# Decoder step with a mixture of experts: the way from routing to the first expert reordered, the overflow branch moved behind the last expert

## The chip, the cores and the metric

One Trainium2 chip, one of its cores. The metric is device time in microseconds (us) of one execution; lower is better. Engines: TensorE (PE; PEld is its weight load), VectorE (DVE), ScalarE (ACT), GpSimd (POOL), SyncE (SP, which only issues DMAs).

## The reference, cut to what matters

544 tokens (512 of a prompt, 32 of a sample group), width 1024, all fp32. After attention, convolution and memory attention each token has a row h; hn is h normalised. A router picks 4 of 32 experts per token, and each expert is a clamped SwiGLU:

```python
logits = (x @ w_router) + b_router                 # x = rmsnorm(h), 544 rows
top_v, top_e = lax.top_k(logits, 4)
gates = softmax(top_v)
h_ = xb @ w_gate_up[e] + b_gate_up[e]              # per expert, on its own tokens
gate = minimum(h_[:, 0::2], 7); up = clip(h_[:, 1::2], -7, 7)
y_e = ((up + 1) * gate * sigmoid(1.702 * gate)) @ w_down[e] + b_down[e]
y = rmsnorm(h + sum over the 4 experts of gates * y_e) * g_final
```

## The kernel before, in words

The kernel has two stages. The first, up to about 235 us, computes h and hn, row tile by row tile (4 tiles of 128 tokens, one of 32), and writes them to two tables in DRAM, y_tbl and hn_tbl (SP, lines 517 and 519). The second goes through the 32 experts, each as one block of at most CAP = 104 tokens. If an expert has more tokens, 20 more blocks are computed at the end; the 0/1 value flag_i says whether any has. With the inputs timed here it is 0.

Between the stages stands the routing. For expert 0, VectorE writes the one-hot matrix hot (which token sits in which slot, line 1526). TensorE multiplies it by the token numbers (line 2441). VectorE turns the result into row numbers idx_i (line 1641). GpSimd gathers these rows of hn_tbl with an indirect DMA (gather, line 737). TensorE transposes the gathered rows (x_rows, line 2355), ScalarE rounds them to the high part (x_high, line 1127), and VectorE computes the low part (x_low, line 1754). Then TensorE begins the products of expert 0. The weight of each token in its sum, its gate, is computed on VectorE by gates (lines 1510 to 1513, 1500, 1501), brought into slot order by a second product with hot (info, line 2342; for expert 0 line 2447) and reduced by slot_info (line 1658) to the column gcol. For later experts slot_info also writes the row numbers (line 1657).

An expert's weights are 12 halves of 128x2048 fp32. A 2 MB chunk (two halves) comes by one SP DMA (line 444) into one of 6 buffers. For each half ScalarE makes the high part (high_part, line 1098, one of 4 buffers), VectorE the low part (low_part, line 1690: raw minus high), and TensorE does three products for each piece (lines 2371 to 2373: high times high, high times low, low times high), 12 products for a half of gate_up. The code numbers the halves 0 to 11 within a period; the periods before the first, with n = -1, hold halves 10 to 13, which are the first four halves of expert 0. So gate_up(-1, 10) is the first product of the second stage, and low_part(-1, 10) the low part that it needs.

The order on every engine is written out by hand: head(0), then period(n) for each expert, with semaphores between engines. head(0) on VectorE is slot_info(0, 0), low_part 10, hot_slots(1, 1) (line 1648), x_low(0), low_parts 11, 12 and 13, and slot_info(1, 1), which gives the row numbers of expert 1. x_rows(1) comes on TensorE after the sixth half of period 0.

Before head(0) every engine reads flag_i into a register (value_load), behind the semaphore route_ready. VectorE branches on it: the overflow code (some 200 instructions) or one memset (line 1745). Then it sets route_ready (line 1748). "spare" (line 1910) is a product of the identity with itself that nobody reads; one shows as two instructions.

Of the kernel before, what the change touches and what calls it, by code (L numbers as in the profile page):

```python
# [112 lines left out]
def build(nc, x_prompt, x_sample, mem_prompt, cache_win_k, cache_win_v, win_kT, mem_kT, cache_mem_v,  # L113
# [4 lines left out]
    with ctx:  # L118
# [174 lines left out]
        ssl, rsl = small[:, 190:192], small[:, 192:194]  # L293
        sink8 = small[:, 172:182]
# [128 lines left out]
        def _(sp):  # L423
# [106 lines left out]
            sp.wait_ge(sem("route_ready"), 1)  # L530
            flag = sp.value_load(flag_i[0:1, 0:1], min_val=0, max_val=1)
# [31 lines left out]
            with sp.Fori(2, NE // UB - 1) as it:  # L563
                for u in range(UB):
                    refills(it * UB + u)
            for n in range(NE - UB, NE - 2):
                refills(n)
# [25 lines left out]
            with sp.If(flag > 0):  # L593
                sp.wait_ge(sem("st_y"), 16 * NTT)
                sp.wait_ge(sem("ld_yl"), 16)
                e = sp.value_load(eid_i[0:1, 0:1], min_val=0, max_val=NE - 1)
# [32 lines left out]
        def _(pool):  # L629
# [63 lines left out]

            pool.wait_ge(sem("group_pe"), 2)
# [14 lines left out]

            bound = pool.alloc_register("bound")  # L710
            pool.wait_ge(sem("eid_zero"), 1)
            none = pool.value_load(eid_i[0:1, EXTRA:EXTRA + 1], min_val=0, max_val=0)
# [74 lines left out]
            pool.wait_ge(sem("gates_ready"), 3)  # L787
            head(0)
            pool.wait_ge(sem("route_ready"), 1)
            flag = pool.value_load(flag_i[0:1, 0:1], min_val=0, max_val=1)  # L790
# [31 lines left out]

            for u in range(UB):
                period(NE - UB + u, u, u == UB - 1, u < 2, u == 2)
# [3 lines left out]
            with pool.Else():  # L828
                head(NE)
# [8 lines left out]
        def _(ac):  # L838
# [299 lines left out]
            def head(m):  # L1138
                if m:
                    for i in (10, 11, 12):  # L1140
                        high_part(m - 1, i, True)
                else:
                    ac.wait_ge(sem("pos_pe"), NTT + 2)
                bias_seed(m, 0)
                x_high(m)
                high_part(m - 1, 13, True)
                bias_seed(m, 1)
                high_part(m - 1, 14, True)
                bias_seed(m, 2)
                bias_seed(m, 3)  # L1150
# [60 lines left out]
            for par, n in ((0, 3), (1, 2)):  # L1211
                ac.wait_ge(sem(f"st_h{par}"), 16 * n)
                ac.wait_ge(sem(f"st_hn{par}"), 16 * n)
            for i in (10, 11, 12):
                high_part(-1, i, True)
            ac.wait_ge(sem("route_ready"), 1)
            flag = ac.value_load(flag_i[0:1, 0:1], min_val=0, max_val=1)
# [3 lines left out]
            with ac.Fori(2, NE // UB - 1) as it:  # L1221
                for u in range(UB):
                    period(it * UB + u, u)
            for u in range(UB):
                period(NE - UB + u, u, u == UB - 1)
# [5 lines left out]
            with ac.Else():  # L1231
                ac.wait_ge(sem("w_used"), NE * HALVES)
                head(NE)
# [14 lines left out]
        def _(dv):  # L1248
# [390 lines left out]
            gates(NTT - 2, NTT - 1, P, 2)  # L1639
            dv.wait_ge(sem("pos_pe"), NTT + 1)  # L1640
            v.tensor_scalar(idx_i[0:CAP, 0:1], banks[6][0:CAP, 416:417], float(NT), None, ALU.add).then_inc(sem("idx_ready"), 1)
            gates(NTT - 1, NTT, NSM, 3)
# [49 lines left out]
            link(v.tensor_copy(cnt, banks[0][:, 160:192]))  # L1692
            link(v.tensor_reduce(wk[:, 9, 0:1], cnt, AX.X, ALU.max))
            link(v.tensor_scalar(wk[:, 9, 1:2], wk[:, 9, 0:1], CAP + 0.5, None, ALU.is_gt))
            link(v.tensor_copy(flag_i[:, :], wk[:, 9, 1:2]))
            flag = dv.value_load(flag_i[0:1, 0:1], min_val=0, max_val=1)

            with dv.If(flag > 0):

                for par, n in ((0, 3), (1, 2)):  # L1700
                    dv.wait_ge(sem(f"st_hn{par}"), 16 * n)
                c0 = chain[0]
# [39 lines left out]

                skipped = chain[0] - c0
            with dv.Else():
                v.memset(eid_i[:, 0:EXTRA], 0).then_inc(sem("dve_chain"), skipped)
            dv.wait_ge(sem("dve_chain"), chain[0])

            v.memset(mx, 0.0).then_inc(sem("route_ready"), 1)
# [27 lines left out]

            def head(m):
                if m:
                    for i in (10, 11):
                        low_part(m - 1, i, True)  # L1780
                if not m:
                    slot_info(0, 0, again=False)
                    low_part(m - 1, 10, True)
                else:
                    hot_slots(m, 0)
                    slot_info(m, 0)
                hot_slots(m + 1, 1)
                x_low(m)
                if not m:
                    low_part(m - 1, 11, True)  # L1790
# [48 lines left out]
            def period(n, k, last=False, table=False, bare=False):  # L1839
                old = not (last or table or bare)  # L1840
                for i in range(10 if last else HALVES):
# [13 lines left out]
                    if not last or i + 2 < 10:  # L1855
                        low_part(n, i + 2, last)
                    if i == 0 and old:
# [18 lines left out]
            head(0)  # L1876
            for u in range(2 * UB):
                period(u, u)
            with dv.Fori(2, NE // UB - 1) as it:
                for u in range(UB):  # L1880
                    period(it * UB + u, u, table=True)
            for u in range(UB):
# [4 lines left out]
            with dv.Else():  # L1887
                dv.wait_ge(sem("w_used"), NE * HALVES)
                head(NE)
# [14 lines left out]
        def _(pe):  # L1904
# [440 lines left out]
            def x_rows(n, k):  # L2345

                pe.wait_ge(sem("gathered"), n * 16 + 16)
                if isinstance(n, int) and n in (0, NE):
# [57 lines left out]
            def head(m):  # L2406
                if m:
                    info(m, 0)
                x_rows(m, 0)
                pe.wait_ge(sem("x_low"), m * 2 + 2)  # L2410
                gate_up(m - 1, 10, True, 0)
                gate_up(m - 1, 11, True, 0)
# [48 lines left out]
            for u in range(UB):  # L2461
                period(NE - UB + u, u, u == UB - 1, u < 2, u == 2)
            with pe.If(flag > 0):
                head(NE)
# [56 lines left out]
```

## Time and profile before

| what | value |
|---|---|
| median of 3 runs | 1386.02 us (1385.52 to 1387.04) |
| the profiled execution | 1385.96 us |
| its span in the trace | 1384.1 us |
| mean granted TensorE clock | 0.995 |
| TensorE busy | 1352.9 us (98% of the span) |
| VectorE, ScalarE, GpSimd busy | 1209.8, 1091.7, 1010.1 us |
| DMA, mean | 332 GB/s |

The profiled execution took 1.9 us more than its span; that part lies outside the first and last instruction. Positions in the trace are given as microseconds from the start of the span. A busy time is the union of the engine's instructions. In the chain, each piece is what released the next.

### The profile page before, as it was taken

Reading aid. Unit: us, or ns where it says so; the run is one execution under the profiler, and the core shown is the slowest. Engines: PE = TensorE matmul, PEld = TensorE weight load, DVE = VectorE, ACT = ScalarE, POOL = GpSimd, SP = SyncE. Lnnn points to the kernel's source line nnn. Section 1 sums busy time; section 2 is a strip of 40 time slices with the busy share of each in tenths; the row PEclk is TensorE's granted clock in tenths of the full one; section 3 lists DMA queues with packets and bytes.
Section 4 is the critical chain, followed back from the end, with each engine's and each line's share of the span. In section 5 each row is a group of like instructions: output and inputs, shape, how many; then the busy total and the mean of one; then the engine's idle time right before and its main releaser. Section 6 shows DMA issues by size and latency. Waiting matters only on the chain.

```text
span 1384.1 us, 19701 instructions
## 1 busy us (share of the span) xinstructions
PE 1352.9 (98%) x6762; PEld 994.0 (72%) x6762; DVE 1209.8 (87%) x1092; ACT 1091.7 (79%) x1149; POOL 1010.1 (73%) x431
## 2 busy tenths in 40 slices
PE   8999999999999999999999999999999999999995
PEld 5988655667777777777777777777777777777773
DVE  5466556899999999999999999999999999999996
ACT  5354423778888888888888888888888888888885
POOL 2122211266699999899999998999999989999943
PEclk9999999999999999999999999999999999999998
DMA  9522272999999999999999999999999999999984
GB/s 354 189 66 72 88 276 70 367 394 356 372 351 377 378 369 382 372 392 379 377 393 373 378 382 375 379 384 365 389 380 365 381 390 374 382 371 386 375 313 150
DMA packets 51803, 458.99 MB, mean 332 GB/s; under 512 B 11450, under 2 KB 15516, under 8 KB 26122
## 3 DMA queue, kind: packets, MB, share of 16 engines
q1 hardware_dynamic: 40089, 438.33, 80.9%
q0 software_dynamic: 10000, 18.19, 6.0%
q10 hardware_dynamic: 1648, 1.65, 0.4%
q8 instruction: 36, 0.59, 0.2%
q14 instruction: 30, 0.24, 0.0%
HBM read 446.62 MB, written 22.08 MB: 339 GB/s over the span
## 4 chain that ended last, share of the span: by engine, by line
PE 77%; DMA 3%; DVE 1%; issue 1%; POOL 1%; ACT 0%; POOLq 0%; ACTq 0%; DVEq 0%
PE psum L2371 24%; PE psum L2373 24%; PE psum L2372 24%; DMA area<-hn_tbl,idx_i 3%; PE psum L2355 2%; PE psum L2366 2%; POOL small L810 0%; DVE low L1690 0%; PE psum L2342 0%; DVE area L1812 0%; POOL area L695 0%; DVE area L1772 0%; DVE ring L1836 0%; DVE area L1765 0%; POOL out L820 0%
## 5 line engine op out<-in xcount | busy, mean ns | idle before, releaser
L1690 DVE TENSOR_TENSOR low<-raw,high 128x2048 fp32r<-128x2048 f32 x384 | 875.1, 2310 | 35.9 <-ACT high L1098 35.8
L1098 ACT CAST high<-raw 128x2048 fp32r<-128x2048 f32 x384 | 727.8, 1913 | 23.7 <-PE psum L2373 19.2
L2371 PE MATMUL psum<-high,area_r 128*104 128x512 f32 x1536 | 610.4, 397 | 2.5 <-DVE area_r L1754 1.4
L2373 PE MATMUL psum<-low,area_r 128*104 128x512 f32 x1536 | 604.3, 393 | 0.0
L2372 PE MATMUL psum<-high,area_r 128*104 128x512 f32 x1536 | 603.9, 393 | 0.0
L668 POOL PARTITION_BROADCAST brow<-brow x192 | 382.8, 2074 | 41.1 <-DMA brow<-in_biases 40.6
L2373 PEld LDWEIGHTS psum<-low,area_r 128*104 128x104 f32 x1536 | 258.0, 168 | 96.5
L2371 PEld LDWEIGHTS psum<-high,area_r 128*104 128x104 f32 x1536 | 258.0, 168 | 95.0 <-DVE area_r L1754 1.6
L2372 PEld LDWEIGHTS psum<-high,area_r 128*104 128x104 f32 x1536 | 258.3, 168 | 90.7
L737 POOL DMA_INDIRECT area<-hn_tbl,idx_i x32 | 162.9, 5089 | 79.5 <-DVE idx_i L1657 40.8
L665 POOL COPY arrived<-cst 1x1 f32 x60 | 199.5, 3325 | 0.3
L747 POOL DMA_INDIRECT y_tbl<-area,idx_i x31 | 160.1, 5164 | 12.7 <-issue 6.4
L1136 ACT COPY psum<-brow 104x512 f32<-104x512 f32 x192 | 110.9, 589 | 4.9 <-POOL brow L668 4.1
L645 POOL TENSOR_TENSOR ring<-ring,small 128x512 f32<-128x512 f32 (+2 forms) x18 | 24.2, 1358 | 80.4 <-DVE small L1364 80.4
L1122 ACT CAST area_r<-psum 128x416 fp32r<-128x416 f32 x64 | 32.4, 505 | 58.4 <-PE psum L2366 58.4
L1112 ACT ACTIVATE area<-psum,cst 104x512 f32<-104x512 f32 x64 | 44.1, 688 | 31.8 <-PE psum L2373 31.8
L721 POOL DMA_INDIRECT slot_tbl<-wr,us x20 | 58.0, 2899 | 5.4 <-issue 5.4
L2129 PE MATMUL psum<-ring,area 128*128 128x512 f32 x112 | 52.4, 601 | 0.0
L728 POOL CAST idx_i<-us 104x1 int32 (+1 forms) x22 | 19.3, 876 | 43.0 <-PE psum L2373 43.0
L1118 ACT ACTIVATE area<-area,cst 104x512 f32<-104x512 f32 x64 | 47.0, 735 | 2.7
L1106 ACT ACTIVATE area<-psum,area 104x512 f32<-104x512 f32 x62 | 39.3, 685 | 12.5 <-PE psum L2373 12.5
L1759 DVE TENSOR_TENSOR area_r<-psum,area_r 128x416 fp32r<-128x416 f32 x64 | 37.6, 588 | 11.7 <-ACT area_r L1122 11.6
(269 smaller groups left out, 1175.5 us busy)
## 6 DMA issues: line engine op xcount, KB each, us to landing
raw<-in_w_gate_up SPq DMA_DIRECT2D x128, 2048.0 KB, 11.1
raw<-in_w_down SPq DMA_DIRECT2D x64, 2048.0 KB, 11.7
ring<-in_w_in SPq DMA_DIRECT2D x7, 1024.0 KB, 15.3
ring<-in_x_prompt SPq DMA_DIRECT2D x8, 512.0 KB, 9.7
ring<-in_w_out SPq DMA_DIRECT2D x7, 512.0 KB, 4.6
ring<-in_w_mem_kv SPq DMA_DIRECT2D x2, 1024.0 KB, 9.3
ring<-in_mem_kT SPq DMA_DIRECT2D x1, 2048.0 KB, 8.5
ring<-in_cache_mem_v SPq DMA_DIRECT2D x1, 2048.0 KB, 8.2
```

Of the source, the lines that this page charges most:

```text
L665: nc.gpsimd.tensor_copy(arrived[0:1, part:part + 1], seen[:, bass.ds(n, 1), 0])
L668: nc.gpsimd.partition_broadcast(brow[:, cols], brow[0:1, cols], channels=P).then_inc(sem("bias_cast"), 1)
L721: nc.gpsimd.indirect_dma_start(slot_tbl[:, :], bass.IndirectOffsetOnAxis(ap=slot_i[0:n, i:i + 1].bitcast(U32), axis=0), slot_row[0:n, i, : ...
L737: nc.gpsimd.indirect_dma_start(xg[0:CAP, k % 2, :], None, hn_tbl[:, :], bass.IndirectOffsetOnAxis(ap=idx_i[0:CAP, k % UB:k % UB + 1].bitca ...
L747: nc.gpsimd.indirect_dma_start(y_tbl[:, :], bass.IndirectOffsetOnAxis(ap=idx_i[0:CAP, (k - 1) % UB:(k - 1) % UB + 1].bitcast(U32), axis=0) ...
L1098: nc.scalar.copy(high_w(i), raw_w(t)).then_inc(sem("w_high"), 1)
L1136: nc.scalar.copy(banks[q][0:CAP, :], brow[0:CAP, q * 512:(q + 1) * 512]).then_inc(sem("spare_bias_in"), 1)
L1690: v.tensor_tensor(low_w(t), raw_w(t), high_w(i), ALU.subtract).then_inc(sem("w_low"), 1)
L2129: last = mm(bank[0:n, :], zT[:, t, j * P:j * P + n], wo[t][:, half * 512:(half + 1) * 512], start=(t == tiles[0]), stop=(t == tiles[-1]))
L2371: mm(bank, high, wh, start=False, stop=False, skip_group_check=True)
L2372: mm(bank, low, wh, start=False, stop=False, skip_group_check=True)
L2373: return mm(bank, high, wl, start=False, stop=stop, skip_group_check=True)
```

## The change

It has six parts. One thing serves them all: `counted`, a semaphore set by the copy of the counts.

1. The flag is read late. On ScalarE, VectorE, GpSimd and SP the read stands before the last four experts, on TensorE after the last. VectorE computes it there (overflow_flag). The overflow code moves into the branch at the end.
2. GpSimd reads the constant `none` before it clears xg, not between the arrival of hn_tbl and the gather. It no longer waits for gates_ready.
3. ScalarE starts the high parts when VectorE has written hn (hn_ready), not when the stores of h and hn have landed. It waits for gates_ready before high part 13.
4. VectorE copies the counts out of PSUM, writes the row numbers of expert 0, and then goes: low_part 10, low_part 11, gates of the last two row tiles, x_low(0), hot_slots(1, 1), low_part 12, slot_info(0, 0), low_part 13; slot_info(1, 1) follows the first low part of period 0.
5. TensorE does the six wide products that stood behind route_ready behind `counted`, and the product of the gates (info(0, 0)) between the first and the second half of expert 0.
6. 12 spare products stand before the transposes of expert 0 (where 8 stood, and 5 stay ahead), and 6 between them and the first half.

```diff
 # sp
-            sp.wait_ge(sem("route_ready"), 1)
-            flag = sp.value_load(flag_i[0:1, 0:1], min_val=0, max_val=1)
...
+            sp.wait_ge(sem("flag_ready"), 1)
+            flag = sp.value_load(flag_i[0:1, 0:1], min_val=0, max_val=1)
 # gpsimd
+            bound = pool.alloc_register("bound")
+            pool.wait_ge(sem("eid_zero"), 1)
+            none = pool.value_load(eid_i[0:1, EXTRA:EXTRA + 1], min_val=0, max_val=0)
             pool.wait_ge(sem("group_pe"), 2)
             nc.gpsimd.memset(xg, 0.0).then_inc(sem("zeroed"), 1)
...
             for par, n in ((0, 3), (1, 2)):
                 pool.wait_ge(sem(f"st_hn{par}"), 16 * n)
-
-            bound = pool.alloc_register("bound")
-            pool.wait_ge(sem("eid_zero"), 1)
-            none = pool.value_load(eid_i[0:1, EXTRA:EXTRA + 1], min_val=0, max_val=0)
...
             gather(0, 0)
-            pool.wait_ge(sem("gates_ready"), 3)
             head(0)
-            pool.wait_ge(sem("route_ready"), 1)
-            flag = pool.value_load(flag_i[0:1, 0:1], min_val=0, max_val=1)
 # scalar
                 x_high(m)
+                if not m:
+                    ac.wait_ge(sem("gates_ready"), 3)
                 high_part(m - 1, 13, True)
...
-            for par, n in ((0, 3), (1, 2)):
-                ac.wait_ge(sem(f"st_h{par}"), 16 * n)
-                ac.wait_ge(sem(f"st_hn{par}"), 16 * n)
+            ac.wait_ge(sem("hn_ready"), NTT + 1)
             for i in (10, 11, 12):
                 high_part(-1, i, True)
-            ac.wait_ge(sem("route_ready"), 1)
-            flag = ac.value_load(flag_i[0:1, 0:1], min_val=0, max_val=1)
             head(0)
 # vector
             first_slots(NTT - 2, NTT).then_inc(sem("hot_ready"), 1)
-            gates(NTT - 2, NTT - 1, P, 2)
+            v.tensor_copy(cnt, banks[0][:, 160:192]).then_inc(sem("counted"), 1)
             dv.wait_ge(sem("pos_pe"), NTT + 1)
             v.tensor_scalar(idx_i[0:CAP, 0:1], banks[6][0:CAP, 416:417], float(NT), None, ALU.add).then_inc(sem("idx_ready"), 1)
-            gates(NTT - 1, NTT, NSM, 3)
...
+            def first_head():
+                low_part(-1, 10, True)
+                low_part(-1, 11, True)
+                gates(NTT - 2, NTT - 1, P, 2)
+                gates(NTT - 1, NTT, NSM, 3)
+                x_low(0)
+                hot_slots(1, 1)
+                low_part(-1, 12, True)
+                slot_info(0, 0, again=False)
+                low_part(-1, 13, True)
...
+                    if isinstance(n, int) and n == 0 and i == 0:
+                        slot_info(1, 1)
...
-            head(0)
+            first_head()
...
+            overflow_flag()
+            dv.wait_ge(sem("flag_ready"), 1)
+            flag = dv.value_load(flag_i[0:1, 0:1], min_val=0, max_val=1)
 # tensor, head(0)
                 x_rows(m, 0)
+                if not m:
+                    for _ in range(6):
+                        mm(banks[5][:, 0:P], ident, ident, start=False, stop=True, skip_group_check=True)
                 pe.wait_ge(sem("x_low"), m * 2 + 2)
                 gate_up(m - 1, 10, True, 0)
+                if not m:
+                    pe.wait_ge(sem("gates_ready"), 3)
+                    info(0, 0)
                 gate_up(m - 1, 11, True, 0)
 # tensor, before head(0)
             spare(5, banks[1], ident)
-            pe.wait_ge(sem("gates_ready"), 3)
+            pe.wait_ge(sem("counted"), 1)
+            for q in range(6):
+                last = mm(banks[q][0:CAP, :], hot[:, 0, 0, :], hot[:, 0].rearrange("p j s -> p (j s)")[:, 0:512], start=True, stop=True)
+            last.then_inc(sem("pos_pe"), 1)
             pe.wait_ge(sem("idx_ready"), 1)
-            for j in range(NTT):
-                last = mm(banks[6][0:CAP, 416:420], hot[:, 0, j, :], rv_all[:, 0, j, :], start=(j == 0), stop=(j == NTT - 1))
-            last.then_inc(sem("info_pe"), 1)
-            spare(8, banks[1], ident)
-            pe.wait_ge(sem("route_ready"), 1)
-            flag = pe.value_load(flag_i[0:1, 0:1], min_val=0, max_val=1)
-            for q in range(6):
-                last = mm(banks[q][0:CAP, :], hot[:, 0, 0, :], rv_all.rearrange("p n j c -> p (n j c)")[:, 0:512], start=True, stop=True)
-            last.then_inc(sem("pos_pe"), 1)
+            spare(12, banks[7], ident)
             head(0)
```

## Rows read from the trace of the kernel before

**Rows 1.** The page: span, and busy time of each engine.
```profile
span 1384.1 us, 19701 instructions
PE 1352.9 (98%) x6762; PEld 994.0 (72%) x6762; DVE 1209.8 (87%) x1092; ACT 1091.7 (79%) x1149; POOL 1010.1 (73%) x431
```

**Rows 2.** The waits of TensorE from 262 us on: total, times, longest.
```profile
PE psum L2355 <- DMA area<-hn_tbl,idx_i: 3.6, 2, 3.0
```

**Rows 3.** The chain of waits, 228 to 262 us: start, duration, what.
```profile
236.96 0.50 POOLq L712
...
238.21 0.96 issue
239.17 5.17 DMA area<-hn_tbl,idx_i
...
246.69 0.48 PE psum L2371
...
254.03 0.39 PE psum L2342 x5
...
255.52 16.51 DMA area<-hn_tbl,idx_i
```

**Rows 4.** The timeline of VectorE around the first expert: start, duration, instruction.
```profile
234.15 0.73 DVE L1477 SCALAR_TENSOR_TENSOR area<-ring,small 32x512 f32<-32x512 f32 x1
...
235.63 0.18 DVE L1510 TENSOR_TENSOR ring<-ring 128x32 f32<-128x32 f32 x1
...
236.86 0.15 DVE L1641 TENSOR_SCALAR idx_i<-psum 104x1 int32<-104x1 f32 x1
...
237.97 0.21 DVE L1501 TENSOR_TENSOR area_r<-area,area_r 32x32 fp32r<-32x32 f32 x1
...
240.47 0.07 DVE L1745 MEMSET eid_i<- 128x20 int32 x1 [1.59 <-issue]
...
257.38 2.28 DVE L1690 TENSOR_TENSOR low<-raw,high 128x2048 fp32r<-128x2048 f32 x1
```

**Rows 5.** The timeline of ScalarE, same stretch.
```profile
234.26 0.23 ACT L994 ACTIVATE ring<-ring 32x32 f32<-32x32 f32 x1 [1.87 <-DVE ring L1495]
237.02 5.51 ACT L1098 CAST high<-raw 128x2048 fp32r<-128x2048 f32 x3 [2.54 <-DMA hn_tbl<-area]
```

**Rows 6.** The timeline of GpSimd: the gathers of experts 0, 1 and 2.
```profile
239.17 1.39 POOL L737 DMA_INDIRECT area<-hn_tbl,idx_i  x1 [4.95 <-issue]
255.52 5.10 POOL L737 DMA_INDIRECT area<-hn_tbl,idx_i  x1 [14.96 <-DVE idx_i L1657]
...
287.88 9.94 POOL L737 DMA_INDIRECT area<-hn_tbl,idx_i  x1 [12.79 <-PE psum L2373]
```

**Rows 7.** A later gather on GpSimd and VectorE beside it, in one timeline.
```profile
1222.27 5.68 POOL L737 DMA_INDIRECT area<-hn_tbl,idx_i  x1 [0.88 <-DMA brow<-in_biases]
...
1222.47 4.49 DVE L1690 TENSOR_TENSOR low<-raw,high 128x2048 fp32r<-128x2048 f32 x2
```

**Rows 8.** Stretches: length, busy time of PE, PEld, DVE, ACT, POOL; clock; DMA.
```profile
241.00:244.00 3.00, 1.63 (x6) 0.93 (x6) 2.55 (x2) 2.12 (x2) 0.00 (x0) 1.00 0.40 105
244.00:247.50 3.50, 1.74 (x12) 1.36 (x13) 1.96 (x3) 2.49 (x3) 0.00 (x0) 1.00 0.59 154
247.50:251.00 3.50, 3.50 (x10) 2.40 (x9) 3.50 (x3) 0.71 (x2) 0.00 (x0) 0.51 1.01 431
```

**Rows 9.** The timeline of TensorE: spare products, wide products, transposes.
```profile
238.72 2.03 PE L1910 MATMUL psum<-cst 128*128 128x128 f32 x16
241.59 1.63 PE L2453 MATMUL psum<-area_r 128*104 128x512 f32 x6 [0.85 <-DVE small L1748]
```

**Rows 10.** The timeline of VectorE at the change from expert 27 to 28.
```profile
1227.37 8.89 DVE L1690 TENSOR_TENSOR low<-raw,high 128x2048 fp32r<-128x2048 f32 x4
1237.59 2.29 DVE L1690 TENSOR_TENSOR low<-raw,high 128x2048 fp32r<-128x2048 f32 x1 [1.32 <-ACT high L1098]
```

**Rows 11.** The timeline of ScalarE, same stretch.
```profile
1240.03 0.69 ACT L1112 ACTIVATE area<-psum,cst 104x512 f32<-104x512 f32 x1 [0.67 <-PE psum L2373]
```

More of the change, by code:

```diff
@@ L293, in build @@
         ssl, rsl = small[:, 190:192], small[:, 192:194]
+        most = small[:, 194:196]
         sink8 = small[:, 172:182]
@@ L595, in _ @@
                 sp.wait_ge(sem("ld_yl"), 16)
+                sp.wait_ge(sem("route_ready"), 1)
                 e = sp.value_load(eid_i[0:1, 0:1], min_val=0, max_val=NE - 1)
@@ L821, in last_store @@
                                              bounds_check=bound, oob_is_err=False).then_inc(sem("st_last"), 16)
+            pool.wait_ge(sem("flag_ready"), 1)
+            flag = pool.value_load(flag_i[0:1, 0:1], min_val=0, max_val=1)
             for u in range(UB):
@@ L828, in _ @@
             with pool.Else():
+                pool.wait_ge(sem("route_ready"), 1)
                 head(NE)
@@ L1223, in _ @@
                     period(it * UB + u, u)
+            ac.wait_ge(sem("flag_ready"), 1)
+            flag = ac.value_load(flag_i[0:1, 0:1], min_val=0, max_val=1)
             for u in range(UB):
@@ L1232, in _ @@
                 ac.wait_ge(sem("w_used"), NE * HALVES)
+                ac.wait_ge(sem("route_ready"), 1)
                 head(NE)
@@ L1690, in low_part, with overflow_flag, overflow_blocks @@
                 v.tensor_tensor(low_w(t), raw_w(t), high_w(i), ALU.subtract).then_inc(sem("w_low"), 1)
[L1692 to L1702, printed above, removed]
+            def overflow_flag():
+                link(v.tensor_reduce(most[:, 0:1], cnt, AX.X, ALU.max))
+                link(v.tensor_scalar(most[:, 1:2], most[:, 0:1], CAP + 0.5, None, ALU.is_gt))
+                v.tensor_copy(flag_i[:, :], most[:, 1:2]).then_inc(sem("flag_ready"), 1)
+            def overflow_blocks():
                 nb, ci, cx, t0 = (wk[:, r, 0:NE] for r in (9, 10, 11, 6))
@@ L1741, in _ @@
                 link(gate_parts(P, 0, NTT, NE, NE + EXTRA))
[L1743 to L1748, printed above, removed]
+                v.memset(mx, 0.0).then_inc(sem("route_ready"), 1)
             def x_low(n):
@@ L1775, in swiglu @@
                 v.scalar_tensor_tensor(out=u, in0=u, scalar=1.0, in1=g, op0=ALU.add, op1=ALU.mult).then_inc(sem("glu_ready"), 1)
-            def head(m):
[L1778 to L1786, printed above, removed]
+            def first_head():
[8 more added lines that the diff above has]
+                low_part(-1, 13, True)
+            def head(m):
+                for i in (10, 11):
+                    low_part(m - 1, i, True)
+                hot_slots(m, 0)
+                slot_info(m, 0)
                 hot_slots(m + 1, 1)
                 x_low(m)
-                if not m:
-                    low_part(m - 1, 11, True)
                 low_part(m - 1, 12, True)
@@ L1888, in _ @@
                 dv.wait_ge(sem("w_used"), NE * HALVES)
+                overflow_blocks()
                 head(NE)
@@ L2347, in x_rows @@
                 pe.wait_ge(sem("gathered"), n * 16 + 16)
-                if isinstance(n, int) and n in (0, NE):
+                if isinstance(n, int) and n == NE:
                     pe.wait_ge(sem("gcol_ready"), counted(n) + 1)
@@ L2462, in _ @@
                 period(NE - UB + u, u, u == UB - 1, u < 2, u == 2)
+            pe.wait_ge(sem("flag_ready"), 1)
+            flag = pe.value_load(flag_i[0:1, 0:1], min_val=0, max_val=1)
             with pe.If(flag > 0):
+                pe.wait_ge(sem("route_ready"), 1)
                 head(NE)
```

## The prediction, made before the changed kernel ran

> **What bounds the kernel.** I read the page first. TensorE is busy for 1352.9 of 1384.1 us, 98%, and no other engine is above 87% [rows 1]. The reader is to see that a microsecond counts only if TensorE's stream of products starts earlier or waits less. Next I read TensorE's waits from 262 us on. Gathers end two of them, together 3.6 us, the longest 3.0 us [rows 2]. So the second stage is a nearly closed stream, and the change can gain or lose only at its start, in these waits, or by cutting a new hole.
>
> Then I read the chain around the start [rows 3]. The store of hn lands at 236.96, GpSimd reads its constant, the gather of expert 0 starts at 239.17 and lands 5.17 us later, at 244.34, and the first product starts at 246.69. From landing to first product are 2.35 us: transposes, high part, low part. The chain does not pass through the flag, the branch or the gates. The timelines show why: VectorE has its row numbers at 236.86 + 0.15 = 237.01 and is through the gates at 237.97 + 0.21 = 238.18 [rows 4], long before 244.34. The branch costs VectorE an idle 1.59 us [rows 4] and TensorE an idle 0.85 us before the wide products [rows 9], both under the gather's flight. Taking the flag away is by itself worth nothing on the chain.
>
> The windows add one thing. TensorE's clock was granted in full up to 247.5. From 247.5 to 251.0 it was at 0.51, the 1.2 GHz level, after the engine had been busy for 1.63 of 3.00 and 1.74 of 3.50 us [rows 8]. Half rate for 3.5 us costs about 1.7 us.
>
> **The parts, costed.**
>
> GpSimd's constant (part 2). Before, 2.21 us pass from 236.96 to the gather at 239.17, with the last 0.96 us "issue" [rows 3]. Without the load the issue stays: 237.92 and thus **-1.25 us** for the start. The row numbers don't hold it: with the gates moved behind them they come earlier than 237.01. The expert 1 gather shows the same distance: TensorE's product starts at 254.03 and takes 0.39 us, and 255.52 is 1.1 us after that [rows 3], with VectorE's 0.15 us instruction between.
>
> ScalarE and VectorE start sooner (parts 3 and 4). ScalarE's last small job ends at 234.49, and it then waits for the store until 237.02 [rows 5]. VectorE's last write of hn ends at 234.15 + 0.73 = 234.88 [rows 4]. So the high parts start near 234.9. Three take 5.51 us [rows 5], 1.84 each: done at 236.8, 238.6 and 240.4. VectorE then does low part 10 from 236.9 and low part 11 without a gap, to 241.4 (two in 4.49 us [rows 7]). In the first stage's end this looks free: VectorE was idle there.
>
> It is not free, because **the gather now starts inside these two low parts**. GpSimd's gather instruction takes 1.39 us for expert 0, when VectorE does nothing long, 5.10 us for expert 1 and 9.94 us for expert 2 [rows 6]. The reader should lay each beside VectorE's timeline. The gather of expert 1 starts at 255.52 and ends at 260.62; the low part that starts at 257.38 ends at 259.66 [rows 4], 0.96 us before. The gather at 1222.27 ends at 1227.95; the two low parts beside it end at 1226.96 [rows 7], 0.99 us before. Every gather I laid beside VectorE this way ends about 1.0 us after the first gap in a run of instructions that read two SBUF tiles. So the gather of expert 0 will start at 237.9, find its gap after low part 11 at about 241.5, and end at 242.5, where it ended at 240.56: **+1.95 us** (this holds the -1.25 us already). Its unknown is bounded by 1.39 us (not held, end at 239.3) and 9.94 us (end at 247.9). I take 4.6 us, because low part 11 is followed by the short instructions of the gates, which read one tile every second time.
>
> Here a page speaks. The Trainium skill, in "SBUF — State Buffer", section "Who interferes with whom", says that a tensor_tensor with two SBUF inputs contends with GpSimd's reads, and infers that writing the descriptors of a DMA is not touched by it. By its inference gathers would not be stretched by low parts, the landing would be near 243.1 and the kernel faster (second rival). The trace disagrees with the inference by 5.10 and 9.94 against 1.39 us [rows 6], and the measurement decides.
>
> From the end of the gather instruction to the landing were 244.34 - 240.56 = 3.8 us; the load is the same, so it lands at 246.3. With 2.35 us behind it the first product is at 248.6, **+1.95 us**. The gates take 237.97 + 0.21 - 235.63 = 2.55 us [rows 4], now from 241.4 to 244.0, before x_low needs VectorE at about 247.2: nothing. If the gather were quick they would end just before x_low: nothing to +0.3.
>
> Gates' product between the halves (part 5). Five short products took 0.39 us in the same place one half later [rows 3]: **+0.4 us** on TensorE. Below nothing is excluded, it is an addition; above, if gates or high part 13 were late, +1. High part 13 waits for x_high anyway.
>
> Spare products (part 6). Sixteen instructions took 2.03 us [rows 9], so a spare product is 0.25 us. The twelve, with five and the six wide products (1.63 us [rows 9]) before them, keep TensorE busy to about 242.3, and it then idles until 246.3: nothing on the chain. The six last 1.5 us inside the 1.4 us that TensorE waits for x_low: 0 to +0.1, up to +0.7 if the clock falls among them. The clock's part: before, 3.5 us at half rate all fell on products. Now TensorE idles for 4 us in one piece, so I expect the fall too, but the first 1.1 us of it on spare products: **-0.4 us**. The bounds are -1.7 (no fall) and +1.3 (a fall that starts with the products and lasts longer).
>
> slot_info(1, 1) behind a low part (part 4). It releases the gather of expert 1, 255.52 before. Counting on from a first product at 248.6: VectorE's low part 13 waits for slot_info(0, 0), so for TensorE, and the next low part ends near 257.3, the gather starts near 258.4. But now only one low part stands in its way, not one and a half, so its instruction ends at 261.4 against 260.62. TensorE reaches the transposes of expert 1 about 1.9 us later than before and had waited a little there. The gather lands 1 to 2 us later: they meet. I count **-0.1 us**. What is late next is the gather of expert 2, held 9.94 us [rows 6] and followed by the 3.0 us wait [rows 2]. It is started by VectorE's slot_info, which moves along with TensorE, so the wait stays: 0.
>
> The late flag (part 1). VectorE has four low parts from 1227.37 on without a gap; the third ends near 1234.0 and there the flag goes in: three short instructions, 0.6 us, and the load, 1.59 us [rows 4]. The fourth then ends at 1238.5, not 1236.26. After it VectorE idled 1.32 us [rows 10]. TensorE needs it when it has done the second half of expert 28, at 1240.03 [rows 11]. Cover 1.5 us: nothing; without the cover +0.7, on ScalarE's side too. SP and GpSimd have a half's time to spare. TensorE's load is behind its last product, and removing the branch on VectorE moves nothing as shown above.
>
> **The sum.** +1.95 + 0.4 - 0.4 - 0.1 = +1.85 us. Against the profiled execution, 1385.96 us, that is 1387.8. It stands 0.06 us from the median of 1386.02, so the forecast is 1387.8 for the median too. About 0.2%, or 2.8 us, is what a measurement of this kernel can tell from no change.
>
> **The rivals.**
>
> First, the forecast: the gather of expert 0 is held by the low parts. Chance 0.50.
>
> Second, it is not held (it gets in before VectorE, or a gap opens between the two low parts). Then -1.25 at the start, +0.4 for the gates' product, and no long idle, so the clock may stay full: up to -1.7. The sum is -2.5, of which the gather of expert 1 and the DMA traffic may take back one: 1383.5 to 1385, likeliest 1384. For it speaks that the forecast counts 1 us steps; against it all three gathers of rows 6. Chance 0.22.
>
> Third, it is held, but the shift opens a gap for the gather of expert 2. Its 9.94 us [rows 6] shrink and the 3.0 us wait [rows 2] goes: 1387.8 - 3.0 = 1384.8. Against it: VectorE, ScalarE and TensorE shift together. Chance 0.10.
>
> Fourth, the other side, slower beyond measurement: the clock. TensorE idles 4 us before the transposes. If the clock is at half from the transposes through the whole first half of weights, its 12 products take 5.1 us for 2.75, so 2.35 us are lost where 1.7 were, and the six spare products overrun by 0.7: +1.85 + 0.4 + 0.65 + 0.7 = +3.6, 1389.6. It decides from a fall before 246.5 on. Chance 0.12.
>
> Fifth, the late flag cuts a hole of 1 to 2 us: 1389. Chance 0.06.
>
> **How the numbers follow.** The likeliest case gives 1387.8. The range takes in the second and third rival and the fourth: 1383.2 to 1389.8. Faster by over 0.2% (below 1383.2) needs the second rival's best or two lucky ones: 0.14. Slower by over 0.2% (above 1388.8) is the fourth, part of the fifth and the worse bounds of the first: 0.19. The rest, 0.67, is within.
>
> **What would show it.** Right: the gather of expert 0 starts near 237.9 and its instruction lasts 4 to 5 us, ending 1 us after low part 11; the first product comes at 248 to 249; a clock stretch near 0.5 of 2 to 3.5 us; the 3.0 us wait is still there; no wait of TensorE near 1240. Wrong: a gather instruction of 1 to 2 us with landing at 243 (second rival), a gather of expert 2 much below 9.9 us (third), transposes of 0.2 us a piece (fourth).

## The result and the profile after

The changed kernel is slower: 1389.72 us median of 22 runs (1384.21 to 1391.95) against 1385.61 us (1383.92 to 1387.59, 22 runs) of the kernel before. The ratio is 1.0025, 95% interval 1.0017 to 1.0032, so +3.5 us; the two medians lie 4.1 us apart. The forecast was +1.85 us, 1387.8, in a range (1383.2 to 1389.8) that holds the median by 0.08 us; but I gave "within 0.2%" 0.67 and "slower" only 0.19, and slower it is.

The profiled execution took 1387.46 us, one of the quicker ones. The reader must know this before he compares the traces: it shows the start of the trouble and not its usual size. Among the 22 runs the mean granted clock goes with the time, but loosely: 1384.2 us at 0.996, 1387.1 to 1387.7 at 0.995, 1388.2 to 1390.8 at 0.992, 1390.1 to 1391.9 at 0.990; yet 1385.7 to 1389.6 at 0.994 and 1387.9 to 1392.0 at 0.991.

First the page of the changed kernel, then its chain around the first expert (start, duration, what).

```profile
span 1385.6 us, 19736 instructions
PE 1358.0 (98%) x6782; PEld 999.2 (72%) x6782; DVE 1209.6 (87%) x1090; ACT 1091.7 (79%) x1149; POOL 1000.5 (72%) x431
```

```profile
235.88 1.90 DMA hn_tbl<-area
...
238.37 0.96 issue
239.33 6.11 DMA area<-hn_tbl,idx_i
245.49 1.40 PE psum L2357 x8
246.89 2.53 PE psum L2414 x12
249.41 0.23 PE psum L2373
```

VectorE's timeline of the same execution:

```profile
235.12 0.73 DVE L1479 SCALAR_TENSOR_TENSOR area<-ring,small 32x512 f32<-32x512 f32 x1
...
237.94 4.49 DVE L1691 TENSOR_TENSOR low<-raw,high 128x2048 fp32r<-128x2048 f32 x2 [0.41 <-ACT high L1099]
...
246.77 1.28 DVE L1746 TENSOR_TENSOR area_r<-psum,area_r 128x416 fp32r<-128x416 f32 x2 [1.93 <-ACT area_r L1128]
```

TensorE's timeline:

```profile
245.49 1.40 PE L2357 MATMUL psum<-cst,area 104*128 104x104 f32 x8 [2.85 <-DMA area<-hn_tbl,idx_i]
...
249.14 0.51 PE L2373 MATMUL psum<-high,area_r 128*104 128x512 f32 x1
```

VectorE's last write of hn is at 235.12 where it was at 234.15 [rows 4]. This 0.97 us is there from about 20 us on, long before anything that the change touches, so I take it off ("stage 1 taken off" from here on). Then the gather starts at 238.4 instead of 239.17 [rows 3], lands at 244.5 instead of 244.34, and the first product is at 248.2 (249.14 in TensorE's timeline) instead of 246.69. From landing to first product were 2.35 us and are 3.7. The chain shows why: it now runs through the six spare products (L2414), which take 2.53 us. VectorE's x_low ends at 246.77 + 1.28 = 248.05, 1.1 us before the first product. The spares, meant for the wait for x_low, outlast it. The windows of the changed kernel (columns as in rows 8) show why:

```profile
244.00:247.50 3.50, 2.01 (x12) 2.02 (x13) 1.36 (x6) 1.08 (x3) 0.00 (x0) 0.76 0.44 87
247.50:251.00 3.50, 3.50 (x18) 3.05 (x17) 3.36 (x3) 2.22 (x2) 0.00 (x0) 0.76 0.90 365
```

The clock was at half from about 245.8 to 249.2, after TensorE had idled 2.85 us before the transposes. In the kernel before this stretch lay on products [rows 8]; here on transposes and spares. GpSimd's timeline, gathers of experts 0 to 2:

```profile
239.33 2.17 POOL L738 DMA_INDIRECT area<-hn_tbl,idx_i  x1 [3.82 <-issue]
258.10 2.96 POOL L738 DMA_INDIRECT area<-hn_tbl,idx_i  x1 [16.61 <-DVE idx_i L1658]
...
289.04 9.94 POOL L738 DMA_INDIRECT area<-hn_tbl,idx_i  x1 [12.80 <-PE psum L2375]
```

The gather of expert 0 took 2.17 us, more than 1.39 [rows 6] but far from 4.6. The question was whether this profile or my reckoning was the exception.

In the next section three executions in a slow state are left out everywhere: one of the changed kernel run again (2472.66 us) and two of the kernel without the six spares (2743.46 and 1500.97 us).

### The profile page after: what moved, and what is told of

The parts are those of the page before. It is cut to its first block, busy times and chain, and to the rows that moved or that the text cites. A ratio compares the mean times of both kernels' runs of the same rounds, so it can differ in the third digit from the quotient of the medians.

```text
span 1385.6 us, 19736 instructions
## 1 busy us (share of the span) xinstructions
PE 1358.0 (98%) x6782; PEld 999.2 (72%) x6782; DVE 1209.6 (87%) x1090; ACT 1091.7 (79%) x1149; POOL 1000.5 (72%) x431
## 4 chain that ended last, share of the span: by engine, by line
PE 88%; DVE 7%; issue 2%; DMA 1%; ACT 1%; POOL 1%; SPq 0%; POOLq 0%; DVEq 0%; ACTq 0%
PE psum L2373 23%; PE psum L2375 23%; PE psum L2374 23%; DVE low L1691 4%; PE psum L2131 4%; PE psum L1968 2%; PE psum L1970 2%; PE psum L1969 2%; PE psum L2357 2%; PE psum L2368 1%; PE psum L1933 1%; DMA ring<-in_w_mem_kv 1%; PE psum L1985 0%; PE psum L2065 0%; PE psum L2041 0%
## 5 line engine op out<-in xcount | busy, mean ns | idle before, releaser
L748 POOL DMA_INDIRECT y_tbl<-area,idx_i x31 | 157.3, 5075 | 12.1 <-issue 6.4
L1767 DVE SCALAR_TENSOR_TENSOR area<-area 104x512 f32<-104x512 f32 x64 | 45.9, 717 | 2.2
```

The source lines that it names most:

```text
L748: nc.gpsimd.indirect_dma_start(y_tbl[:, :], bass.IndirectOffsetOnAxis(ap=idx_i[0:CAP, (k - 1) % UB:(k - 1) % UB + 1].bitcast(U32), axis=0) ...
```

## The experiments

The expectations speak of two theories. Hold theory: GpSimd's gather instruction is kept waiting by VectorE's low parts, and the rows land late. Clock theory: TensorE's clock falls to half around the first expert, and what it does there takes longer.

The medians are of 8 to 12 runs, each beside runs of the kernel before in the same call (33 to 35, median 1386.12 to 1386.17 us). "Gather 0" is the duration of the gather instruction of expert 0 in the one profiled execution.

| kernel | median us | ratio to before (95%) | gather 0, us |
|---|---|---|---|
| changed, again | 1389.38 | 1.0022 (1.0013 to 1.0031) | 4.24 |
| changed, no six spares | 1390.58 | 1.0031 (1.0021 to 1.0041) | 4.24 |
| changed, 24 spares | 1387.41 | 1.0003 (0.9993 to 1.0012) | 4.24 |
| changed, ScalarE waits | 1386.20 | 1.0001 (0.9992 to 1.0009) | 1.39 |
| changed, gates first | 1386.15 | 1.0004 (0.9995 to 1.0012) | 1.39 |
| gates first, their product early | 1385.00 | 0.9995 (0.9987 to 1.0004) | 1.39 |
| the same, 16 spares | 1385.79 | 0.9999 (0.9989 to 1.0009) | 1.39 |
| before, late flag alone | 1387.77 | 1.0012 (1.0004 to 1.0021) | 1.39 |
| the same again | 1388.62 | 1.0019 (1.0008 to 1.0030) | 3.33 |
| the same, 14 spares | 1388.71 | 1.0015 (1.0006 to 1.0025) | 3.34 |
| before, constant early | 1385.42 | 0.9996 (0.9988 to 1.0005) | 1.39 |
| constant early and 9 spares | 1386.62 | 1.0004 (0.9992 to 1.0015) | 1.39 |

**The changed kernel again.** No edit.

> The changed kernel once more, on the chip of the next three. Clock theory: the 22 runs of it spread from 1384.2 to 1392.0 us because TensorE's clock falls around the first expert for a stretch whose length differs from run to run (mean granted clock 0.990 to 0.996); so here again a median of 1388 to 1391, mean clocks of 0.990 to 0.995, and in a profile of a slow run a longer half-rate stretch after 245 us than the 3.7 us of the first profile. Hold theory (the gather held by the low parts costs it): the gather instruction of expert 0 would take over 4 us in slower runs, clock or not.

1389.38 us, as before. Its profiled execution took 1390.81 us, and so shows the loss at its usual size. VectorE, GpSimd and TensorE, from one timeline each:

```profile
235.44 0.23 DVE L1523 SCALAR_TENSOR_TENSOR ring<-psum,ring 128x64 f32<-128x64 f32 x1 [0.39 <-PE psum L2199]
...
237.31 4.48 DVE L1691 TENSOR_TENSOR low<-raw,high 128x2048 fp32r<-128x2048 f32 x2
```
```profile
238.92 4.24 POOL L738 DMA_INDIRECT area<-hn_tbl,idx_i  x1 [4.20 <-issue]
```
```profile
246.81 1.60 PE L2357 MATMUL psum<-cst,area 104*128 104x104 f32 x8 [4.34 <-DMA area<-hn_tbl,idx_i]
248.21 2.53 PE L2414 MATMUL psum<-cst 128*128 128x128 f32 x12
250.50 0.48 PE L2373 MATMUL psum<-high,area_r 128*104 128x512 f32 x1
```

The line of the kernel before that fits the first of these:

```profile
234.84 0.22 DVE L1521 SCALAR_TENSOR_TENSOR ring<-psum,ring 128x64 f32<-128x64 f32 x1
```

The two low parts run to 241.79; the gather instruction starts inside them and ends at 243.16. So it is held, for 4.24 us. With this execution's own stage 1 taken off (0.6 us, 235.44 for 234.84; TensorE's clock was at half from about 233.3 to 236.7 us in it), the rows land 1.8 us later than in the kernel before. TensorE has idled 4.34 us by then, and transposes and spares run at half rate. The first product, at 250.5, is 3.2 us later than before. My expectation put the longer time down to a longer half-rate stretch here, and it was about as long as in the first profile (3.4 us). Both theories are at work, and the hold is what makes TensorE idle.

**Without the six spares**, to see whether they do harm.

```diff
-                if not m:
-                    for _ in range(6):
-                        mm(banks[5][:, 0:P], ident, ident, start=False, stop=True, skip_group_check=True)
```

> The changed kernel without the six spare products between the transposes and the first half. Clock theory in its first form (the spares run at half rate and overrun x_low): the first product comes 1.1 us sooner where the clock has fallen, at x_low's end, but the half-rate stretch then falls on real products; net -1 to +1 us against the changed kernel. If the six spares themselves bring on the longer stretches: -2 to -3 us. Hold theory: no change.

Not faster but 1.2 us slower in the medians: 1390.58 us. The first product comes 0.65 us sooner (stage 1 taken off, here 0.44 us), but the half rate now falls on real products. TensorE's timeline, then its windows:

```profile
249.69 0.75 PE L2373 MATMUL psum<-high,area_r 128*104 128x512 f32 x1 [1.22 <-DVE area_r L1746]
```
```profile
247.50:251.00 3.50, 2.28 (x9) 1.65 (x8) 2.55 (x4) 3.00 (x4) 0.00 (x0) 0.50 0.93 286
251.00:254.00 3.00, 3.00 (x9) 2.06 (x8) 1.44 (x1) 0.30 (x1) 0.00 (x0) 0.58 1.02 437
```

**24 spares before the transposes**, to keep TensorE busy while the gather stays held.

```diff
-            spare(12, banks[7], ident)
+            spare(24, banks[7], ident)
```

> The changed kernel with 24 spare products instead of 12 before the transposes of expert 0, so that TensorE is busy until about 245.5 us, where it idled for 2.9 us. Clock theory: no fall, or a much shorter one, clock 0.995 to 0.997 in all runs, first product near 247.6 us of the profile, and 3 to 5 us faster than the changed kernel, 1385 to 1387. Hold theory: the landing is unchanged and so is the time, within 1 us.

1387.41 us, 2.0 us under the changed kernel in the medians, though its gather is held just as long (4.24 us). TensorE, and its windows:

```profile
241.75 5.52 PE L1912 MATMUL psum<-cst 128*128 128x128 f32 x48
247.24 0.93 PE L2357 MATMUL psum<-cst,area 104*128 104x104 f32 x8
```
```profile
244.00:247.50 3.50, 3.50 (x33) 3.34 (x32) 0.47 (x3) 0.00 (x0) 0.00 (x0) 1.00 0.30 88
247.50:251.00 3.50, 3.50 (x26) 2.94 (x25) 2.60 (x4) 3.14 (x4) 0.00 (x0) 1.00 0.77 225
```

No idle time, full clock, transposes in 0.93 us. That fits the clock theory. But this profile took 1389.11 us, one of the slower executions of its kernel, and its clock had been at half earlier, from about 234.3 to 241.2 us. So the 2 us are measured in the medians; that the clock gives them is read from one profile.

**ScalarE waits for the stores again**, so that low part 10 comes later.

```diff
             ac.wait_ge(sem("hn_ready"), NTT + 1)
+            for par, n in ((0, 3), (1, 2)):
+                ac.wait_ge(sem(f"st_h{par}"), 16 * n)
+                ac.wait_ge(sem(f"st_hn{par}"), 16 * n)
```

> The changed kernel with ScalarE again waiting for the stores of h and hn before its high parts, so that low part 10 begins near 239.9 us instead of 237.9, after the start of the gather instruction (239.3). Hold theory: the gather instruction falls from 2.2 to 1.4 us, it lands 0.8 us sooner, total -0.8 us; but low part 11 and the gates then end near 247, close to x_low, which may cost up to 1 us. Clock theory: the idle stretch before the transposes stays near 2 us, the clock falls as before, total within 1.5 us of the changed kernel.

1386.20 us: all of the loss is gone, more than I had expected of it. The low parts start at 239.04, 0.67 us after the gather at 238.37, and it takes 1.39 us:

```profile
239.04 4.49 DVE L1694 TENSOR_TENSOR low<-raw,high 128x2048 fp32r<-128x2048 f32 x2 [2.48 <-ACT high L1099]
```
```profile
238.37 1.39 POOL L738 DMA_INDIRECT area<-hn_tbl,idx_i  x1 [3.82 <-issue]
```

**Gates first**: the same collision avoided in another way.

```diff
             def first_head():
-                low_part(-1, 10, True)
-                low_part(-1, 11, True)
                 gates(NTT - 2, NTT - 1, P, 2)
                 gates(NTT - 1, NTT, NSM, 3)
+                low_part(-1, 10, True)
+                low_part(-1, 11, True)
```

> The changed kernel with the two gates calls ahead of low parts 10 and 11 on VectorE, so that the gather instruction of expert 0 starts beside the short instructions of the gates and not inside the two low parts. Hold theory together with the clock theory: the gather instruction takes 1.4 to 2 us instead of 4.2, lands near 243.5 to 244 us, TensorE idles under 2 us before it, the clock does not fall on transposes or spares, first product near 246.5 (counted from the same stage 1), and the total is 3 to 4 us under the changed kernel, 1385 to 1386.5. Rival (the low parts have nothing to do with it, the clock falls for another reason): gather and time as in the changed kernel, 1389 to 1390.

As the hold theory said: 1386.15 us, gather 1.39 us, landing 243.4. The low parts start 0.62 us after the gather. The first product, at 245.76, is the earliest of all profiles, 1.0 us before that of the kernel before (stage 1 taken off, 0.11 us). This profile is of the quickest of its 12 executions, 1384.51 us, so that lead does not stand for the median, which is that of the kernel before:

```profile
239.10 4.47 DVE L1691 TENSOR_TENSOR low<-raw,high 128x2048 fp32r<-128x2048 f32 x2
```
```profile
243.47 0.93 PE L2357 MATMUL psum<-cst,area 104*128 104x104 f32 x8 [1.70 <-DMA area<-hn_tbl,idx_i]
244.24 1.52 PE L2414 MATMUL psum<-cst 128*128 128x128 f32 x12
```

**The gates' product early as well.**

```diff
-                if not m:
-                    pe.wait_ge(sem("gates_ready"), 3)
-                    info(0, 0)
                 gate_up(m - 1, 11, True, 0)
...
+            pe.wait_ge(sem("gates_ready"), 3)
+            info(0, 0)
             spare(12, banks[7], ident)
```

(with slot_info(0, 0) between low parts 10 and 11, and x_rows(0) waiting for it as before.)

> As the kernel with gates first, and the product of the gates (five short products) back in front of the twelve spares, in TensorE's idle time, instead of between the first and the second half of expert 0. Both theories: the same start as gates first, and 0.4 us less on TensorE's stream; total 0 to 0.6 us under the kernel with gates first.

1385.00 us, the lowest median of all. The ratio of 0.9995 can't be told from 1, nor from gates first.

**The same with 16 spares** (`spare(12, ...)` to `spare(16, ...)`).

> The kernel with gates first and the gates' product early, with 16 spare products instead of 12 before the transposes. It idles about 1.3 us there; clock theory: filling it takes away the last falls of the clock, 0 to -1 us against its sibling with 12 (1385.0), so 1384 to 1385. If the spares outlast the landing: up to +0.3.

1385.79 us, no gain. The profiles show that there was nothing left to fill: in both kernels with the early product TensorE's clock was at half from about 234.6 to 241.4 us, its spares ran later for it, and the transposes followed them without a gap (at 244.89 with 12 spares, at 245.78 with 16).

**The late flag alone** in the kernel before: part 1 with everything else in its old order, the counts copied behind the gates, the wide products behind `counted`. (The two waits for gates_ready, on GpSimd and ScalarE, stay as in the changed kernel.)

> The kernel before with part 1 of the change alone: the flag computed and read before the last four experts, the overflow code in the last branch, the counts copied behind the gates; everything else in the old order. If the late flag costs nothing (its place is covered): VectorE starts low part 10 about 1.6 to 2 us sooner and the wide products need not wait, the landing decides the start as before: total within 0.5 us of before. Rival (it cuts a hole near 1236 us): +1 to +2 us, with a wait of TensorE on a low part or an act_rows there.

1387.77 us, 1.0012. The expectation of half a microsecond was a miss, and its rival too: TensorE waits for nothing near 1236 us. The first profile did not show the cause, for its gather took 1.39 us. So it ran again, and once with 14 spares instead of 8:

> The kernel with the late flag alone once more, on the chip of the others. Both theories: 1387 to 1388.5 again, if the first figure was no accident; clock theory: in a profile whose clock is full at 236 us, TensorE idles 2 us before the transposes of expert 0, and the clock then falls to half on transposes or first products.

> The kernel with the late flag alone, with 14 spare products instead of 8 before the wide products. Clock theory: without the wait for route_ready, TensorE ran through its spares and wide products sooner and idled about 2 us in one piece right before the transposes; the 6 more spares (1.5 us) fill that, and the 1.6 us that the late flag alone cost go: 1385.5 to 1386.5, equal to before. Rival (the late flag costs its 1.6 us elsewhere, near expert 28 or in code loading): no change, 1387 to 1388.5.

1388.62 and 1388.71 us: the spares are no remedy. The profile of the first of these two shows where the time goes:

```profile
238.96 2.29 DVE L1695 TENSOR_TENSOR low<-raw,high 128x2048 fp32r<-128x2048 f32 x1
```
```profile
239.18 3.33 POOL L738 DMA_INDIRECT area<-hn_tbl,idx_i  x1 [4.96 <-issue]
```
```profile
246.34 0.93 PE L2358 MATMUL psum<-cst,area 104*128 104x104 f32 x8 [4.20 <-DMA area<-hn_tbl,idx_i]
```
```profile
244.00:247.50 3.50, 0.93 (x8) 0.74 (x8) 0.01 (x1) 0.55 (x2) 0.00 (x0) 0.99 0.34 92
247.50:251.00 3.50, 2.36 (x6) 1.70 (x7) 3.50 (x4) 2.66 (x3) 0.00 (x0) 0.50 0.88 304
251.00:254.00 3.00, 3.00 (x9) 2.07 (x8) 3.00 (x2) 0.00 (x0) 0.00 (x0) 0.50 1.02 437
```

In the kernel before, VectorE's timeline has

```profile
240.66 2.28 DVE L1690 TENSOR_TENSOR low<-raw,high 128x2048 fp32r<-128x2048 f32 x1
```

With the flag and its branch gone, low part 10 starts at 238.96 and no longer at 240.66. That is 0.22 us before the gather, whose instruction takes 3.33 us; the rows land 2.0 us later than in the kernel before, TensorE idles 4.20 us, and the clock is at half for about the first 5.6 us of products. In the first profile of this kernel TensorE's clock was already at half at the end of stage 1:

```profile
236.00:240.00 4.00, 4.00 (x23) 4.00 (x22) 2.52 (x15) 2.92 (x2) 0.75 (x1) 0.50 0.09 22
```

It brought slot_info late, low part 10 to 240.58, and so the gather got through:

```profile
240.58 2.28 DVE L1695 TENSOR_TENSOR low<-raw,high 128x2048 fp32r<-128x2048 f32 x1
```

That execution was the quickest of its 11, 1385.56 us; the profiled executions with a held gather took 1389.00 and 1388.77 us. No run took the hold away from this kernel, so its part in the loss is read from profiles. Whether the two collide is settled within a microsecond: a low part 10 that began 0.62 to 0.83 us after the gather (ScalarE's waits, gates first, and the two with the early product) left it at 1.39 us, and one that began 0.22 us before it went with 3.33 us.

**GpSimd's constant early alone** (part 2 in the kernel before).

> The kernel before with GpSimd's constant read ahead of the clearing of xg, nothing else. The profile of the changed kernel shows 1.55 us from the landing of hn to the gather where there were 2.21: the gather starts 0.7 us sooner, is not held (the low part starts at 240.7), lands 0.7 us sooner, and the total is -0.7 us against before (-0.2 to -1.2). If the start of the first product is followed by a fixed wait later (the gather of expert 2): 0.

1385.42 us, -0.7 in the medians as expected, but the interval holds 1. The profile does not show the earlier gather: TensorE's clock was at half from about 233.8 to 244.0 us, the row numbers came late, and the gather started at 239.23, where it was at 239.17 before:

```profile
237.56 0.16 DVE L1641 TENSOR_SCALAR idx_i<-psum 104x1 int32<-104x1 f32 x1
```
```profile
239.23 1.39 POOL L737 DMA_INDIRECT area<-hn_tbl,idx_i  x1 [4.54 <-issue]
```

**The same with 4 spares behind the wide products and 5 behind the transposes.**

> The kernel before with GpSimd's constant read early, 4 spare products behind the wide products (into the 1.2 us idle before the transposes) and 5 between the transposes and the first half (into the 1.4 us wait for x_low). Clock theory: the half-rate stretch of 3.5 us on the first products, seen from 247.5 us in the kernel before, does not come or comes seldom: -1 to -1.7 us against the kernel with the early constant alone (1385.4), so 1383.8 to 1384.5. Rival (clock falls do not hang on these gaps): 1385.4 to 1385.8.

1386.62 us, no gain. In its profile the clock is at half from about 234.4 to 244.6, the products before the transposes are late, and the four spares then stand in the way. So it doesn't decide whether the clock's fall in the kernel before can be had back.

## Why the prediction was right, and where it was not

The number was right by luck. The median of 1389.72 us is 0.08 us inside the upper end of the range, eleven of the 22 executions are above it, and the loss is about twice the forecast.

**The hold** was right in mechanism and size. I had 4.6 us for the gather instruction; three profiles of the changed order have 4.24 us, one has 2.17. The instruction run again ended at 242.6 with stage 1 taken off, where I had 242.5: 1.37 us after the low parts and not 1.0, which themselves ended 0.3 us sooner. In the profile with 2.17 us the gather started 1.39 us after low part 10, in the others 1.61, and it got in between the two low parts. The prediction had claimed that only a gap lets it in. Undoing the overlap in two ways brings the time back to 1.0001 and 1.0004, so the hold is shown to be the root of the loss.

**The constant** was mis-sized: -1.25 us. It gives 0.66: from the landing at 237.78 to the gather at 239.33 are 1.55 us, where 2.21 were. The pieces of "issue" before it stayed, and I had kept only the last. "The row numbers don't hold it" is true of the first profile, but not of every execution: in the changed kernel run again TensorE's clock was at half in the end of stage 1, the row numbers were there at 237.39, and the gather followed them by the same 1.5 us, at 238.92.

**The clock and the six spares** are the step that failed in size. I had 0 to +0.1 for the spares and -0.4 for the clock. Landing to first product took 3.7 us instead of 2.35 in both profiles of the changed kernel: transposes 1.4 to 1.6 for 0.93, spares 2.5 to 2.7 for 1.52. The fourth rival, +3.6 in all with a chance of 0.12, had such an overrun in its price; the measured +3.5 is its time. Its mechanism is only half met: the clock was low on transposes and spares, but back to full with the first products.

Followed onward, the second profile of the changed kernel tells how 3.2 us at the first product become 4.3 at the end. The transposes of experts 1, 2 and 3 stand 1.6, 2.7 and 3.9 us behind those of the kernel before (stage 1 taken off), and from there on the distance stays near that. So about 1.6 us came back before expert 1, since the products there run at the full clock, and at that point the loss was no more than the +1.85 of the forecast. What came on top lies further on, where the sum had 0. It came first in the wait for expert 2's rows, because its row numbers had come late too. VectorE's slot_info, run again and before:

```profile
290.27 0.15 DVE L1658 TENSOR_SCALAR idx_i<-psum 104x1 int32<-104x1 f32 x1
```
```profile
286.79 0.15 DVE L1657 TENSOR_SCALAR idx_i<-psum 104x1 int32<-104x1 f32 x1
```

Behind that wait the clock fell a second time, now on products (windows of the changed kernel run again):

```profile
310.00:316.00 6.00, 3.11 (x18) 2.16 (x17) 5.86 (x10) 2.63 (x5) 5.79 (x5) 0.93 1.01 422
316.00:322.00 6.00, 6.00 (x22) 4.22 (x22) 5.96 (x6) 4.38 (x4) 0.09 (x1) 0.78 0.71 236
```

In the first profile of the changed kernel, and in that of the kernel before, the clock stays at 1.00 there; the first profile is 0.5 us late at the end, net of stage 1. With 24 spares, with ScalarE's waits and with the gates' product early it falls to 0.72 to 0.74 over 310 to 316 us. So the fall goes with no edit I made. It goes with the wait: all four falls follow a wait of 1.9 to 2.9 us that expert 2's rows ended, and none follows the 1.5 us that VectorE ended, in seven profiles. But three waits for the rows, of 3.0 us (before), 2.5 (late flag again) and 2.3 (gates first), had no fall behind them. What decides there I can't say.

**The flag.** "Taking the flag away is by itself worth nothing" is the wrong sentence. The late flag alone costs 1.6 to 2.5 us in the medians (1.0012, 1.0019). I read the idle 1.59 us on VectorE [rows 4] as free because it lay under the gather's flight. By the profiles it lay there as a screen: it kept low part 10 off GpSimd's 1.39 us. I had the mechanism in hand and applied it only to the new order of the low parts. Where the flag now is, no hole came: the low part that starts at 1236.48 is followed by no wait of TensorE.

```profile
1236.48 2.29 DVE L1691 TENSOR_TENSOR low<-raw,high 128x2048 fp32r<-128x2048 f32 x1 [0.96 <-DVE flag_i L1697]
```

**The gates' product** took 0.37 us in the chain, as counted. Moving it back gave 1.15 us in the medians (1386.15 to 1385.00), while the intervals of the two ratios overlap.

**Later gathers.** The gather of expert 1 took 2.96 us for 5.10, as worked out. That of expert 2 kept its 9.94. The wait behind it was counted as fixed at 3.0; it is 1.5 us in the first profile, where VectorE ends it, and 2.9 in the second, where the rows end it. TensorE's waits of the first profile from 262 us on, total, times, longest:

```profile
PE psum L2357 <- DVE area_r L1751: 1.5, 1, 1.5
PE psum L2373 <- DVE area_r L1751: 1.4, 2, 0.9
PE psum L2368 <- DVE area L1767: 0.6, 1, 0.6
```

With stage 1 taken off, the first profile is level with the kernel before at the transposes of expert 1 (273.02 for 272.07), 1.3 us ahead at those of expert 2 (310.39 for 310.73) and level again at those of expert 3 (347.25 for 346.24), so which of the two ends the wait is one reason for the spread. The third rival's event, a shorter gather of expert 2, came only in the old order of VectorE: 7.49 or 7.50 us in four of its six profiles, 9.93 or 9.94 in the other two and in all eight of the new order. It does not give 3.0 us: in those four VectorE ends the wait, after the same 1.5 us.

**The inference of the Trainium skill** ("SBUF — State Buffer", section "Who interferes with whom"), that descriptor writing is not touched by a tensor_tensor, would leave this gather alone, and 4.24 against 1.39 us for the same gather disagree again. The section's first half, contention of two SBUF inputs with GpSimd's reads, fits 3.33 and 4.24 us beside low parts, which read two SBUF tiles. No run tells whether it is the reading of the row numbers or the writing of the descriptors that waits.

Open: why some boundaries between two low parts let the gather in and others do not; what decides whether TensorE's clock is at half in the end of stage 1 (it was in eight of the 14 profiles, by no edit), and whether it falls again after the wait for expert 2; and what a version without any fall of the clock would take.

## What to carry to other kernels

Before you start work earlier on one engine, ask which short operation on another engine used that engine's idle time as a screen: here 1.4 us of GpSimd needed VectorE to have no low part under way. An idle stretch beside the critical path is free only if what will fill it holds up nothing on the path. Spare products that bridge a wait are sized at full clock; here, behind idle stretches of 2.85 and 4.34 us, they ran at half and outlasted the wait, while twelve more of them in the idle stretch before gave 2 us back. And one profile is one execution: the first of the changed kernel and the first of the late flag alone each hid what the median shows.

## What was not expected of the hardware

The same kernel, same data, spreads over 8 us. A gather that started 1.39 us into a pair of low parts took 2.17 us, and three that started at 1.61 us took 4.24. And twelve more spare products, useless work of 2.8 us, made the changed kernel 2 us faster.
